# A depthwise convolution whose tap products are packed into four 32-column strips of TensorE, over copies shifted by way of DRAM

## What is computed

```python
D_MODEL, SEQ, N_META, CONV_WIDTH = 1024, 256, 16, 31

def conformer_conv(h, w_pw1, b_pw1, w_dw, b_dw, ln_g, ln_b, w_pw2, b_pw2):
    u = h @ w_pw1 + b_pw1
    a, gate = jnp.split(u, 2, axis=-1)
    u = a * jax.nn.sigmoid(gate)
    u = lax.conv_general_dilated(
        u, w_dw[:, None, :].astype(u.dtype),
        window_strides=(1,), padding=((CONV_WIDTH - 1, 0),),
        dimension_numbers=("NWC", "WIO", "NWC"),
        feature_group_count=D_MODEL) + b_dw
    u = jax.nn.silu(layer_norm(u, ln_g, ln_b))
    return u @ w_pw2 + b_pw2
...
        hn = rms_norm(h, mix_norm_g[i])
            h = h + conformer_conv(hn, ...)
```

## Time and profile before

| | |
|---|---|
| median of 3 runs | 2121.33 us (2121.14 to 2125.59) |
| profiled execution, its own time | 2124.38 us |
| its span | 2122.6 us |
| TensorE's mean granted clock | 0.986 of full speed |
| TensorE busy | 2051.1 us, 97% of the span |
| VectorE busy | 1526.2 us, 72% |
| ScalarE busy | 1212.9 us, 57% |

### The profile page before, as it was taken

The page is one execution under the profiler, slowest core; times in us unless marked ns, Lnnn a source line. Parts: engine busy times, 40 slices in busy tenths (PEclk is TensorE's granted clock), DMA queues, the critical chain, the costliest instruction groups (busy, mean ns, idle before and its releaser), DMA issues.

```text
span 2122.6 us, 31838 instructions
## 1 busy us (share of the span) xinstructions
PE 2051.1 (97%) x12270; PEld 1803.1 (85%) x12270; DVE 1526.2 (72%) x1721; ACT 1212.9 (57%) x1371; POOL 56.9 (3%) x104
## 2 busy tenths in 40 slices
PE   6989999999999999999999999999989989999997
PEld 5979999888888887888878888889978869989997
DVE  5976654589898887988889898896576157626653
ACT  6554443477777677777767777675354345515442
POOL 2001000000000000000000000001000100020000
PEclk9999999899999999999999999999999989999999
DMA  4214554199898998989989898993532324444551
GB/s 191 80 62 177 179 181 154 58 345 368 325 354 337 345 363 318 369 325 356 347 336 366 329 353 337 343 372 139 182 137 100 125 76 157 159 159 173 185 180 59
DMA packets 70102, 504.19 MB, mean 238 GB/s; under 512 B 7680, under 2 KB 8704, under 8 KB 8832
## 3 DMA queue, kind: packets, MB, share of 16 engines
q1 hardware_dynamic: 70016, 502.95, 63.3%
HBM read 501.87 MB, written 1.05 MB: 237 GB/s over the span
## 4 chain that ended last, share of the span: by engine, by line
PE 89%; DVE 5%; ACT 3%; issue 2%; DMA 1%; POOL 0%; ACTq 0%; DVEq 0%; POOLq 0%; SPq 0%
PE ps L794 9%; PE ps L798 9%; PE ps L797 8%; PE ps L551 8%; PE ps L554 8%; PE ps L555 8%; PE ps L819 5%; PE ps L823 5%; PE ps L822 5%; PE ps L528 3%; PE ps L1079 2%; PE ps L612 2%; PE ps L1082 2%; PE ps L1081 2%; PE ps L755 1%
## 5 line engine op out<-in xcount | busy, mean ns | idle before, releaser
L1747 DVE TENSOR_TENSOR ring_r<-ring,high 128x2048 fp32r<-128x2048 f32 x227 | 517.7, 2289 | 110.6 <-ACT high L1440 93.6
L1440 ACT ACTIVATE high<-ring 128x2048 fp32r<-128x2048 f32 x224 | 428.5, 1913 | 14.8 <-DMA ring<-w_stream 14.8
L1648 DVE TENSOR_TENSOR ring_r<-ring,high 128x2048 fp32r<-128x2048 f32 x120 | 274.8, 2293 | 130.0 <-ACT high L1261 129.6
L797 PE MATMUL ps<-ring_r,big_r 128*128 128x512 f32 x896 | 349.0, 389 | 0.0
L554 PE MATMUL ps<-scr_r,high 128*128 128x256 f32 (+1 forms) x1200 | 343.3, 286 | 0.0
L1261 ACT ACTIVATE high<-ring 128x2048 fp32r<-128x2048 f32 x120 | 228.3, 1907 | 162.4 <-PE ps L551 91.6
L794 PE MATMUL ps<-high,big_r 128*128 128x512 f32 x704 | 287.8, 409 | 0.0
L798 PE MATMUL ps<-high,big_r 128*128 128x512 f32 x704 | 275.5, 391 | 0.0
L1747 DVE TENSOR_TENSOR ring_r<-ring,scr_r 128x2048 fp32r<-128x2048 f32 x112 | 254.6, 2287 | 6.1 <-ACT scr_r L1440 2.4
L551 PE MATMUL ps<-sq_r,high 128*128 128x272 f32 (+1 forms) x832 | 238.7, 287 | 8.2 <-DVE scr_r L1655 8.2
L555 PE MATMUL ps<-sq_r,ring_r 128*128 128x272 f32 (+1 forms) x832 | 237.7, 286 | 0.0
(11 more groups left out here) (424 smaller groups left out, 3808.4 us busy)
## 6 DMA issues: line engine op xcount, KB each, us to landing
ring<-w_stream SPq DMA_DIRECT2D x477, 1024.0 KB, 4.8
h<-h_in SPq DMA_DIRECT2D x1, 1088.0 KB, 5.1
out<-hn SPq DMA_DIRECT2D x1, 1024.0 KB, 4.7
vec<-vec_in SPq DMA_DIRECT2D x1, 576.0 KB, 8.0
```

Source lines behind the costliest of these rows:

```text
L797: pe.matmul(o, x_item_high[:, k, :], w_low[:, cols], start=False, stop=False)
L1440: act.activation(w_high, w, ACT.Copy).then_inc(S["moe_high"], 1)
L1648: dve.tensor_tensor(w_low, blocks_at(c, 0, CH), w_high.bitcast(F32), ALU.subtract).then_inc(S["weights_low"], 1)
L1747: dve.tensor_tensor(w_low, w, w_high.bitcast(F32), ALU.subtract).then_inc(S["moe_low"], 1)
```

## The change

It does six things:
- TensorE's taps become 20 for every tile (`PE_TAPS` = `TURNS` * `TAP_STEPS` = 4 * 5), VectorE's the last 11.
- The operand of TensorE's taps is a new buffer, `shifted`. For each group of 32 channels its 128 partitions hold the same 32 channels four times, shifted by 0, 1, 2 and 3 steps in time. One product of a 128x32 matrix with it makes four taps of 32 channels; five such products, 4 columns apart, make 20 taps. There are four groups of channels (`GROUPS`), so 20 products of 32 output columns a tile, each group writing to its own 32 partitions of bank 6.
- SyncE makes the copies (`shift`): it stores the tile of `conv_u` to a DRAM scratch tensor `spread` (128x302), waits until it has landed, and loads it back in four DMAs (32x4x288 each). The first 12 weight chunks after the ring's first fill are issued in straight code, with `shift(c - 6)` behind chunk `c`, and both of the last two tiles' shifts behind chunk 12. A shift also waits for the loads of the one before.
- The matrices (`diag`) are made by VectorE, in one instruction a tile (128x640); ScalarE's 109 instructions go.
- TensorE takes tile `j` - 2 after `pw1` of tile `j`, and the mean takes tile `j` - 3. Buffers of `diag` and `shifted` are three deep.
- VectorE does its own taps of tile `j` right behind the product of the halves, the bias in with the last sum, and picks bank 6 up in a separate instruction (`take_conv`), tile `j` - 3, ahead of the matrices of step `j`.

The semaphore `h1_ready` is merged into `x_ready`, with its counts moved by 8; this changes no order.

```diff
-PE_TAPS = [13] * 6 + [15, 16]
+TURNS = 4
+GROUPS = P // 32
+TAP_STEPS = 5
+PE_TAPS = TURNS * TAP_STEPS
+CONV_LEN = CONVW - 1 + T0
+SHIFT_LEN = T0 + TURNS * (TAP_STEPS - 1)
...
+            def shift(j):
+                sp.wait_ge(S["glu_done"], j + 1)
+                if j >= 3:
+                    sp.wait_ge(S["conv_done"], j - 2)
+                if j:
+                    sp.wait_ge(S["shift_landed"], 16 * (TURNS + 1) * j)
+                sp.dma_start(spread[j], conv_u[:, j, :]).then_inc(S["shift_landed"], 16)
+                sp.wait_ge(S["shift_landed"], 16 * (TURNS + 1) * j + 16)
+                by_group = spread[j].rearrange("(g c) t -> c g t", g=GROUPS)
+                for s in range(TURNS):
+                    sp.dma_start(shifted[32 * s:32 * s + 32, j % 3, :, :], by_group[:, :, s:s + SHIFT_LEN])\
+                      .then_inc(S["shift_landed"], 16)
...
+            for c in range(RING, 3 * RING):
+                sp.wait_ge(pre_begun, c - RING + 2)
+                sp.dma_start(slot(c), w_stream[c]).then_inc(dense_landed[c % RING], 16)
+                if c - RING < KD - 1:
+                    shift(c - RING)
+                if c - RING == KD - 2:
+                    shift(KD - 1)
...
             def conv_tile(j):
-                pe.wait_ge(S["glu_done"], j + 1)
+                pe.wait_ge(S["shift_landed"], 16 * (TURNS + 1) * (j + 1))
                 pe.wait_ge(S["diag_ready"], j + 1)
                 claim(6)
-                for tap in range(PE_TAPS[j]):
-                    mm = pe.matmul(ps[:, 6, 0:T0], diag[:, j % 2, tap, :], conv_u[:, j, tap:tap + T0],
-                                   start=(tap == 0), stop=(tap == PE_TAPS[j] - 1))
+                for n in range(TAP_STEPS):
+                    for g in range(GROUPS):
+                        mm = pe.matmul(ps[32 * g:32 * g + 32, 6, 0:T0], diag[:, j % 3, g * TAP_STEPS + n, :],
+                                       shifted[:, j % 3, g, TURNS * n:TURNS * n + T0],
+                                       start=(n == 0), stop=(n == TAP_STEPS - 1))
...
-                if j >= 1:
-                    conv_tile(j - 1)
                 if j >= 2:
-                    add_to_mean(j - 2)
+                    conv_tile(j - 2)
+                if j >= 3:
+                    add_to_mean(j - 3)
+            conv_tile(6)
+            add_to_mean(5)
             conv_tile(7)
             add_to_mean(6)
             add_to_mean(7)
...
-                if j >= 2:
-                    act.wait_ge(S["conv_done"], j - 1)
-                for tap in range(PE_TAPS[j]):
-                    ins = act.activation(diag[:, j % 2, tap, :], ident[:, :], ACT.Copy,
-                                         scale=vcol("w_dw", j * CONVW + tap))
-                ins.then_inc(S["diag_ready"], 1)
...
+            def make_diag(j):
+                if j >= 3:
+                    dve.wait_ge(S["conv_done"], j - 2)
+                n = GROUPS * TAP_STEPS
+                dve.tensor_tensor(diag[:, j % 3, :, :], diagonal.unsqueeze(1).broadcast_to([P, n, 32]),
+                                  vcol("w_dw", j * n, n).unsqueeze(2).broadcast_to([P, n, 32]), ALU.mult)\
+                   .then_inc(S["diag_ready"], 1)
...
-                step(dve.tensor_tensor(conv_sum, conv_y[:, j, :], conv_sum, ALU.add))
+                step(dve.scalar_tensor_tensor(out=conv_y[:, j, :], in0=conv_y[:, j, :], scalar=vcol("b_dw", j),
+                                              in1=conv_sum, op0=ALU.add, op1=ALU.add))
+
+            def take_conv(j):
                 dve.wait_ge(S["conv_done"], j + 1)
-                dve.scalar_tensor_tensor(out=conv_y[:, j, :], in0=ps[:, 6, 0:T0], scalar=vcol("b_dw", j),
-                                         in1=conv_sum, op0=ALU.add, op1=ALU.add).then_inc(S["conv_ready"], 1)
-                dve.wait_ge(S["conv_ready"], j + 1)
+                dve.tensor_tensor(conv_y[:, j, :], ps[:, 6, 0:T0], conv_y[:, j, :], ALU.add)\
+                   .then_inc(S["conv_ready"], 1)
 
             for j in range(8):
                 split_weights((BOFF["pw1"] + j * KD + KD - 1) // CH + LOOK)
+                if j >= 3:
+                    take_conv(j - 3)
+                make_diag(j)
                 dve.wait_ge(S["glu_sig"], j + 1)
                 dve.scalar_tensor_tensor(out=conv_u[:, j, CONVW - 1:CONVW - 1 + T0], in0=ps[:, 2 * (j % 3), 0:T0],
                                          scalar=vcol("b_pw1", j), in1=gate_sb[:, j % 2, :],
                                          op0=ALU.add, op1=ALU.mult).then_inc(S["glu_done"], 1)
-                if j >= 1:
-                    conv_dve(j - 1)
-            conv_dve(7)
+                last_taps(j)
+            for j in (5, 6, 7):
+                take_conv(j)
```

More of the change, by code:

```diff
@@ L45 @@
 VECS = [
-    ("b_pw1", 16), ("w_dw", KD * CONVW), ("b_dw", 8), ("ln_g", 8), ("ln_b", 8), ("b_pw2", 8),
+    ("b_pw1", 16), ("w_dw", KD * GROUPS * TAP_STEPS), ("w_dw_last", KD * (CONVW - PE_TAPS)), ("b_dw", 8), ("ln_g", 8), ("ln_b", 8), ("b_pw2", 8),
     ("pool_scale", 8), ("mix_g0", 8), ("mix_g1", 8), ("ffn_g0", 8), ("ffn_g1", 8), ("final_g", 8),
@@ L188, in sem @@
             return ctx.enter_context(nc.semaphore(name))
+        spread = nc.dram_tensor("spread", (KD, P, CONV_LEN), F32).ap()
         ps = ctx.enter_context(nc.psum_tensor("ps", [P, 8, 512], F32))
@@ L222, in vcol @@
             return vec[0:rows, VOFF[name] + j:VOFF[name] + j + n]
-        conv_u = big[:, 0:KD * 302].rearrange("p (k t) -> p k t", k=KD)
+        conv_u = big[:, 0:KD * CONV_LEN].rearrange("p (k t) -> p k t", k=KD)
         conv_y = big[:, 2432:2432 + KD * T0].rearrange("p (k t) -> p k t", k=KD)
-        diag = big[:, 4608:4608 + 2 * max(PE_TAPS) * P].rearrange("p (b t c) -> p b t c", b=2, c=P)
+        diag = big[:, 4608:4608 + 3 * GROUPS * TAP_STEPS * 32].rearrange("p (b n c) -> p b n c", b=3, c=32)
+        shifted = big[:, 7680:7680 + 3 * GROUPS * SHIFT_LEN].rearrange("p (b g t) -> p b g t", b=3, g=GROUPS)
+        diagonal = scr[:, 4352:4384]
+        conv_sum = up_sb[:, 0, :]
         rows_of = ((0, P, META, P - 16), (P - 15, P, P, P - 15), (2 * P - 30, 46, 2 * P - 15, 31))
@@ L262, in program @@
         mean = gate_sb[:, 0, :]
-        conv_sum = up_sb[:, 0, :]
         zo = proj[:, 0:8, :]
@@ L444, in _ @@
                     sp.dma_start(vec[:, :], vec_in).then_inc(S["vec_landed"], 16)
-            turns_pre = C_MOE // RING
-            with sp.Fori(1, turns_pre) as r:
+            def shift(j):
[10 more added lines that the diff above has]
+                      .then_inc(S["shift_landed"], 16)
+            turns_pre = C_MOE // RING
+            for c in range(RING, 3 * RING):
[5 more added lines that the diff above has]
+                    shift(KD - 1)
+            with sp.Fori(3, turns_pre) as r:
                 for n in range(RING):
@@ L641, in _ @@
                            after_split(1) if j == 0 else None)
-                bank_owner[b] = (S["h1_ready"], 2 * j + 1)
-                bank_owner[b + 1] = (S["h1_ready"], 2 * j + 2)
+                bank_owner[b] = (S["x_ready"], 2 * j + 1)
+                bank_owner[b + 1] = (S["x_ready"], 2 * j + 2)
             def ffn(n, norm_i, split_n, t, x_low, hidden_high, hidden_low, b_in, b_out, inside, behind):
@@ L715, in _ @@
                 if m >= 4:
-                    pe.wait_ge(S["x_ready"], m - 3)
+                    pe.wait_ge(S["x_ready"], KD + m - 3)
                 if m == 6:
@@ L733, in turn_tokens @@
                 mm.then_inc(S["xt_done"], 1)
-            pe.wait_ge(S["x_ready"], 8)
+            pe.wait_ge(S["x_ready"], KD + 8)
             turn_tokens(0)
@@ L1331, in _ @@
                     for k in (2 * j - 2, 2 * j - 1):
-                        act.wait_ge(S["h1_ready"], k + 1)
+                        act.wait_ge(S["x_ready"], k + 1)
                         act.activation(sq_r[:, k, :], h[:, k, :], ACT.Copy, scale=vcol("ffn_g0", k))\
@@ L1402, in _ @@
             for k in range(KD):
-                act.wait_ge(S["x_ready"], k + 1)
+                act.wait_ge(S["x_ready"], KD + k + 1)
                 act.activation(hn[:, k, 0:SEQ], x[:, k, :], ACT.Copy, scale=vcol("ffn_g1", k))\
@@ L1685, in _, with last_taps @@
             dve.wait_ge(S["consts_ready"], 2)
-            def conv_dve(j):
+            step(dve.tensor_reduce(diagonal, ident[:, :].rearrange("p (b c) -> p c b", c=32), AX.X, ALU.add))
+            def make_diag(j):
[5 more added lines that the diff above has]
+                   .then_inc(S["diag_ready"], 1)
+            def last_taps(j):
                 dve.wait_ge(S["glu_done"], j + 1)
                 sums = (conv_y[:, j, :], conv_sum)
-                for n, tap in enumerate(range(PE_TAPS[j], CONVW)):
+                for n, tap in enumerate(range(PE_TAPS, CONVW)):
                     u = conv_u[:, j, tap:tap + T0]
-                    w = vcol("w_dw", j * CONVW + tap)
+                    w = vcol("w_dw_last", j * (CONVW - PE_TAPS) + n)
```

(7 more changed lines are left out.)

3 lines of the change are left out of this document (2 added, 1 removed).

## The result

The change ran in 2106.57 us (median of 4 runs, 2104.79 to 2107.19) against 2122.61 for the kernel before in the same series (4 runs, 2121.14 to 2125.59): a ratio of 0.9923, 95% interval 0.9907 to 0.9939, 16.0 us faster.

What follows compares the result with a forecast made beforehand. TensorE, busy throughout its 12.43 us step of the convolution stage, was taken to set the pace, VectorE 1.6 us behind. -17.8 us plus 1.5 for low clock gave -16.3: 2105 from the median 2121.3, range 2101 to 2116.

Steps and rivals of the forecast that it cites:

- TensorE's part: TensorE's step in the convolution stage: with taps on four strips at once at 2.29 us, 8.97 us instead of 12.43.
- The allowance of 0.2 us for the changes of shape: In TensorE's step: 0.20 us added for two changes of product shape, taken from no row.
- The strips have streams of their own: TensorE's taps: records for different column strips need not begin in program order, so four run at once, 2.29 us a tile.
- The objection in the text: TensorE's taps: records beginning strictly in order would allow only two strips at once, 4.58 us a tile, 2116 in all; chance 0.12.
- an estimate of 2.9 us a tile: TensorE's taps by the skill's efficiency, some 3.2 times for four strips: 0.6 us more than taken, 2109 in all.
- VectorE's part: VectorE's step in the convolution stage, with split, pick-up, matrices and its own taps: 8.62 us, 0.35 below TensorE's.
- The start: First steps: bank 6 picked up late, at 60.65 us, then 2.0 us of low clock; step 4 begins at 65.4.
- The detour: SyncE's store and four loads a tile: 7.0 us, 9.5 with the chunk; hidden in the middle, bare at the end.
- the rival of the detour: SyncE's shifts set the pace: 2112 at 10 us a shift, no gain at 11.1, +19 at 13.7; chance 0.14.
- The end: Last tiles: tile 7's copies land at 109.4, mean read at 113.3 us against 131.13, 17.8 us earlier before the low clock.
- the 1.5 us of low clock in the sum: TensorE's pauses ahead of the last two tiles may lower the clock, costing 0.9 to 3.5 us; 1.5 taken.

Runs made afterwards that it cites:

- e1: The change with all 20 tap products of a tile written to one strip, plus one full-width identity product: 2152.16 us, ratio 1.0134 to the kernel before.
- e2: The change with the two loops around the tap products swapped, so ten records in a row go to one strip: 2130.71 us, ratio 1.0039 to the kernel before.
- e9: e8 with the change's 20 taps on TensorE instead of 24: 2105.12 us, ratio 0.9910 to the kernel before.
- e5: The change plus 17 unread products that keep TensorE busy ahead of the taps of tile 1: 2104.78 us, ratio 0.9911 to the kernel before.
- e10: e8 with 28 taps on TensorE and 3 on VectorE: 2100.47 us, ratio 0.9891 to the kernel before.
- e4: The change with 24 taps on TensorE and 7 on VectorE: 2105.31 us, ratio 0.9913 to the kernel before.
- e7: e4 with VectorE's pick-up of bank 6 ahead of the split of the weights: 2102.01 us, ratio 0.9905 to the kernel before.
- e6: The kernel before with the new order alone: full-width products, 13 taps a tile, no detour: 2137.10 us, ratio 1.0065 to the kernel before.
- e11: The change with only the first two pick-ups of bank 6 moved earlier, ahead of the split: 2106.72 us, ratio 0.9917 to the kernel before.
- e8: e7 with separate semaphores for stores and loads, and the last two shifts ahead of chunk 12: 2097.81 us, ratio 0.9873 to the kernel before.
- e3: The change with the detour's stores and loads issued by ScalarE instead of SyncE: 2111.29 us, ratio 0.9942 to the kernel before.

## Why the prediction was right

The forecast was 2105 with a sum of -16.3 us; measured are -16.0 by the medians, -17.2 by the spans and -16.4 by the length of the stage. By its own steps:

- **TensorE's part.** Forecast 8.97 us a step, measured 9.10: `pw1` 6.30 instead of 6.22, taps 2.43 instead of 2.29, mean 0.37 instead of 0.26. The allowance of 0.2 us for the changes of shape, which came from no row, should have been 0.33, and most of it lies outside the taps. Four strips at once is shown by e1 and by the stretches of 0.23 us.
- **The reason given for it was too wide.** "The strips have streams of their own" holds only as far as three waiting records (e2). The objection in the text, strict order, would have cost half; had the loops been nested the other way, my reason would have forecast the same time as here, and been 24 us off. That the nesting of the change stays within the limit is luck, as far as the prediction goes. The limit could have been seen: these rows stand around the two of the earlier trace rows, all of the head in front:

```profile
1830.89 0.38 PE L1165 MATMUL ps<-big,ones 128*64 128x256 f32 x1
...
1831.33 0.27 PE L1166 MATMUL ps<-big,ones 128*64 128x128 f32 x1
...
1831.44 0.27 PE L1166 MATMUL ps<-big,ones 128*64 128x128 f32 x1
```

The next head's record at 1830.90 passes exactly three that wait (1831.11, 1831.33, 1831.44), and it begins 0.01 us behind the fourth ahead of it. "Strict FIFO, no reordering" (the Trainium skill, TensorE: Matmul & The Clock Gate, Part 3) does not agree with the change's row, eight counts a stretch with two records to a strip, nor with e2, which strict order would put at 8.5 us a tile. The same part's 2.38 times for three column tiles gave an estimate of 2.9 us a tile; 9.35 / 2.50 = 3.7 times was measured for four.
- **VectorE's part.** Forecast 8.62 us a step with the pick-up and 8.26 without; measured 8.73 and 8.40 (starts of the splits in e9, where it doesn't wait in this stretch: 41.04, 49.44, then 58.19 to 66.92), 0.11 and 0.14 more. The matrices take 0.82 us as worked out. That the engines are 0.35 us apart came out as 0.26 to 0.29 us of idling on VectorE in steps 5 to 7. So the two are all but one bound: edits that take no work from VectorE brought 1.7 us of stage in e5 and 1.3 in e9, and with 28 taps (e10) VectorE idles 4 us a step and the stage is longer than with 24.
- **The start.** The pick-up of tile 0 ends at 60.46 (60.65 forecast). Counted from the first long split, which came 0.57 us earlier than in the kernel before, that is 0.4 us late: three of VectorE's steps with 0.13 us more each. The low clock behind it costs 4.20 - 2.50 = 1.7 us (2.0), as e5 confirms with 1.7. Step 4 begins at 65.10 (65.4).
- **The detour.** A store lands 2.0 to 5.7 us after its issue (2.7 to 5.2), loads take 110.26 - 105.88 = 4.4 (4.3). In the middle nothing waits for them. The last copies land at 110.26 instead of 109.4 and TensorE waits 0.22 us for them: the rival of the detour was that near, and e4 and e7 show it as soon as VectorE ends sooner.
- **The end.** Halves' product of tile 7 99.36 (99.3), VectorE's taps end 104.78 (104.6), tile 5 picked up 105.25 (105.1). Tile 6 takes 3.99 us instead of 2.50, and the mean is read at 114.16 against 114.8. It looks as if the 1.5 us of low clock in the sum had come true, but they never reached the end. Tile 7 has to wait for its copies, and tile 6 ran slowly inside that wait; in the forecast's own figures too, a tile 6 slowed by 1.5 us would have ended at 109.1, ahead of the copies at 109.4. What took their place is that the copies came late: 79.8 us behind the first long split (110.26 - 30.45) against 78.4 (109.4 - 31.02), 0.6 of these 1.4 us from the later product of the halves and the rest from the store and the loads. Behind the copies it is 3.9 us to the mean, as forecast. So two errors of 1.5 and 1.4 us cancel, and that the sum is within 0.3 us is luck by that much.

Where the rest of TensorE's saving is: 25.2 us less work and 16.4 to 17.0 less time, so 8.3 us of it turned into waiting, nearly all in the 8.04 us ahead of tile 1 and the 3.52 ahead of tile 6. e6 prices the order alone at some 14 us, and the products on four strips, with the 11 taps on VectorE, more than pay for it (e6 to the change, 30.5 us by the medians).

What stays open: why the overlap stops at three records, and what it is that the store and the chunk share. That VectorE's chain explains e9's miss is read from its timeline and from the four stretches beside e11; no run with a shorter VectorE step at 20 taps was made to prove it. Nor was e11 repeated with a pick-up in every step. What else than idle time decides when the clock falls is open too (e7).

## What to carry to other kernels

Products of few output columns are free width: cut so that neighbours in the program go to different strips, and nest the loops so that no more than two records of one strip stand in a row (ten were tried, in e2, and nothing between). When one engine is relieved until a second is all but as long, later edits for the first gain little (1.7 us of stage in e5, 1.3 in e9); take work from the second engine too, which is what 24 taps do, and then clear the last transfer. The two edits that brought 1.3 us with 20 taps (e9) brought 7.5 with 24 (e4 to e8, 83.02 to 75.55). A transfer that is hidden in the middle is bare behind the last tile: keep large loads away from the last small ones, and let an engine that computes nothing wait for them.

## What the runs showed of the hardware

- TensorE starts a record for a free strip past records that wait for theirs, up to three of them (e2: the seventh slot of ten; 6.69 us a tile against 2.50).
- Forty float32 records of 272 columns on four strips of 32 take 2.50 us, on one strip 9.35 us.
- A store of 151 KB lands in 2.1 us where no chunk of 1 MB is on the way (103.80 to 105.88). Where one was issued 0.5 to 2.0 us ahead it takes 3.4 to 5.7 us: 5.7 from the same queue (93.63 to 99.28), 5.5 from another (e3, 95.19 to 100.65).
- Behind idle times of 3.5 us (105.40) and 8.0 us (60.61) TensorE ran at 1.2 GHz for a while, and in e7 behind one of 1.95 us too (48 records in 4.64 us); behind 1.4 and 1.0 us in e8 it stayed at 2.4 GHz, and so it did behind 3.48 us in e7 (48 records in 2.96 us). The length of the idle time alone does not tell.
